# Three parts of the second layer's adaption in a one-core block kernel: summed by VectorE among the attention heads instead of by TensorE

## What is computed

```python
def second_block(x, c, w_ada, b_ada, norm_g, ...):
    c_act = jax.nn.silu(c)                                   # one row of 1024
    for layer in range(DEPTH):
        ada = jnp.einsum('bd,de->be', c_act, w_ada[layer]) + b_ada[layer]      # 3072 numbers
        shift, scale, gate = jnp.split(ada, 3, axis=-1)
        h = rms_norm(x, norm_g[layer]) * (1.0 + scale[:, None, :]) + shift[:, None, :]
        y = even_mixer(h, ...) if layer % 2 == 0 else odd_mixer(h, ...)
        x = x + gate[:, None, :] * y
    return rms_norm(x, final_g)
```

## Time and profile before

| | before |
|---|---|
| median of three runs (lowest, highest) | 1607.51 us (1602.76, 1608.37) |
| the profiled execution | 1602.8 us |
| its span, first to last instruction | 1600.9 us |
| TensorE busy in the span | 1573.0 us (98%) |
| VectorE busy | 875.0 us (55%) |
| ScalarE busy | 454.7 us (28%) |
| mean granted clock of TensorE, share of full | 0.999 |
| bytes moved by DMA | 243.40 MB, mean 152 GB/s |

### The profile page before, as it was taken

The page is one execution under the profiler, slowest core; times in us unless marked ns, Lnnn a source line. Parts: engine busy times, 40 slices in busy tenths (PEclk is TensorE's granted clock), DMA queues, the critical chain, the costliest instruction groups (busy, mean ns, idle before and its releaser), DMA issues.

```text
span 1600.9 us, 25330 instructions
## 1 busy us (share of the span) xinstructions
PE 1573.0 (98%) x10283; PEld 1353.5 (85%) x10283; DVE 875.0 (55%) x1685; ACT 454.7 (28%) x949; POOL 11.5 (1%) x24
## 2 busy tenths in 40 slices
PE   7999999999999999999999999999999999999998
PEld 6878868888899999878876888799999777678887
DVE  5547782222667774455793331566775573535663
ACT  5344323212200001335423301310011464623431
POOL 0000000000000000100000000000000000000000
PEclk9999999999999999999999999999999999999999
DMA  9443352342585455333343343485454834473420
GB/s 297 156 154 105 105 173 94 132 158 65 174 285 162 146 163 194 122 118 106 128 146 109 114 149 105 158 255 167 152 172 152 272 119 158 156 253 124 153 106 27
DMA packets 172373, 243.40 MB, mean 152 GB/s; under 512 B 16830, under 2 KB 95204, under 8 KB 172260
## 3 DMA queue, kind: packets, MB, share of 16 engines
q1 hardware_dynamic: 170660, 238.65, 44.3%
q10 hardware_dynamic: 1600, 3.15, 0.6%
HBM read 240.72 MB, written 1.05 MB: 151 GB/s over the span
## 4 chain that ended last, share of the span: by engine, by line
PE 96%; DVE 1%; ACT 1%; issue 1%; DMA 0%; SPq 0%; DVEq 0%; POOL 0%; ACTq 0%
PE psum L599 45%; PE psum L1408 26%; PE psum L610 4%; PE psum L2558 3%; PE psum L411 2%; PE psum L1184 2%; PE psum L2648 2%; PE psum L444 1%; PE psum L1262 1%; PE psum L427 1%; PE psum L2656 1%; PE psum L1234 1%; PE psum L2515 1%; PE psum L633 1%; PE psum L1219 1%
## 5 line engine op out<-in xcount | busy, mean ns | idle before, releaser
L599 PE MATMUL psum<-hT,ring 128*128 128x256 f32 x2448 | 540.8, 380 | 6.0 <-ACT hT L2755 2.6
L599 PEld LDWEIGHTS psum<-hT,ring 128*128 128x128 f32 x2448 | 461.2, 190 | 77.9 <-issue 15.1
L482 DVE TENSOR_TENSOR psum<-psum,const 128x512 f32<-128x512 f32 (+3 forms) x39 | 22.0, 582 | 123.3 <-PE psum L411 118.1
L599 PE MATMUL psum<-uT,ring 128*128 128x256 f32 x384 | 85.6, 381 | 0.0
L1408 PE MATMUL psum<-hT,ring 128*128 128x128 f32 x704 | 82.3, 275 | 2.7 <-issue 2.7
L1408 PEld LDWEIGHTS psum<-hT,ring 128*128 128x128 f32 x704 | 80.4, 192 | 3.1 <-issue 3.1
L599 PEld LDWEIGHTS psum<-uT,ring 128*128 128x128 f32 x384 | 72.5, 190 | 10.9 <-issue 0.7
L1668 ACT ACTIVATE SCR<-SCR 128x512 f32<-128x512 f32 x22 | 13.9, 630 | 220.9 <-DVEq L2166 220.9
L460 ACT ACTIVATE SCR<-psum,stats 128x128 f32<-128x128 f32 (+2 forms) x128 | 49.5, 398 | 55.2 <-DVE stats L496 55.0
L1440 ACT ACTIVATE G<-psum 128x512 f32<-128x512 f32 x32 | 19.1, 597 | 124.8 <-PE psum L599 124.8
L1926 DVE COPY_PREDICATED SCR<-levels,psum 128x512 f32<-128x512 uint8 x32 | 23.4, 733 | 56.7 <-PE psum L1184 56.0
(11 more groups left out here) (512 smaller groups left out, 2574.4 us busy)
## 6 DMA issues: line engine op xcount, KB each, us to landing
ring<-in_w_in SPq DMA_DIRECT2D x46, 1024.0 KB, 7.3
ring<-in_ffn_w_gate_up SPq DMA_DIRECT2D x88, 512.0 KB, 6.0
ring<-in_w_ada SPq DMA_DIRECT2D x24, 1024.0 KB, 9.9
ring<-in_ffn_w_down SPq DMA_DIRECT2D x16, 1024.0 KB, 7.0
ring<-in_w_in_odd SPq DMA_DIRECT2D x16, 1024.0 KB, 8.4
ring<-in_w_in_even SPq DMA_DIRECT2D x10, 1024.0 KB, 7.3
ring<-in_x_w_kv SPq DMA_DIRECT2D x8, 1024.0 KB, 6.0
ring<-in_ssm_w_glu SPq DMA_DIRECT2D x8, 1024.0 KB, 6.3
```

The source lines that it names most:

```text
L482: ins = nc.vector.tensor_tensor(pick(view), pick(view), mask[:, heads], ALU.add)
L599: ins = nc.tensor.matmul(b[0:width, n * S:n * S + S], w[k // 4][:, k % 4, c0[n]:c0[n] + width], tile(k), start=k == 0, stop=k == kt - 1)
```

## The change

TensorE's eight matmuls for each of the three parts go, as do ScalarE's copies. Instead VectorE multiplies each of the eight tiles of a part's matrix (128 x 512) by its column of `c_wide`, one number per partition, and adds it to a row of 128 x 512 in SBUF: the first tile with one tensor_scalar, the other seven with scalar_tensor_tensor (`sum_ada`, one half of a part at a time). Each instruction waits for the one before it. The halves stand in VectorE's steps 10, 11, 12, 13 and, two of them, 14, ahead of what else stands at the end of these steps. TensorE then sums over the 128 partitions with four matmuls whose moving side is one column of ones (`ada_total`, 128x1), in the places of the transposes, and VectorE adds the bias (`store_ada`). The ring's slots of the three parts are freed by the job za3 and by the sums' semaphore.

```diff
-           7: ["zb1", "zb2"], 8: ["zb3", "silu b"], 9: ["za0"], 10: ["za1"], 11: ["ada11"], 12: ["za2", "part ada11"],
-           13: ["za3", "silu a"], 14: ["ada12", "ada13"], 15: ["part 0", "part ada12", "part ada13"],
+           7: ["zb1", "zb2"], 8: ["zb3", "silu b"], 9: ["za0"], 10: ["za1"], 12: ["za2", "part ada11"],
+           13: ["za3", "silu a"], 15: ["part 0", "part ada12", "part ada13"],
...
+ADA_SUMS = {10: [(1, 0)], 11: [(1, 1)], 12: [(2, 0)], 13: [(2, 1)], 14: [(3, 0), (3, 1)]}
...
     for n in (1, 2, 3):
-        ada(1, n)
+        wide(f"ada1{n}", a["w_ada_2"], 512 * n, 512, "za3", 1)
...
+        def ada_total(n):
+            b = ojobs.begin(pe, f"ada1{n} turned")
+            pe.wait_ge(sig["ada_summed"], 2 * n)
+            row = m["ada_rows"][(6 + n) % ADA_SLOTS]
+            for i in range(4):
+                ins = nc.tensor.matmul(b[:, i:i + 1], row[:, i * P:(i + 1) * P], ones[:, 0:1], start=i == 0, stop=i == 3)
+            ins.then_inc(ojobs.done, 1)
...
-                elif name.startswith("ada"):
-                    n = int(name[4])
-                    ada_copy(1, n, {1: None, 2: None, 3: "04"}[n])
...
+        def sum_ada(n, h):
+            w = ring.arrived(dve, f"ada1{n}.{h}")
+            row = m["ada_rows"][(6 + n) % ADA_SLOTS]
+            for k in range(4):
+                by = m["c_wide"][:, 4 * h + k, 0:1]
+                if h == k == 0:
+                    link(V.tensor_scalar(row, w[:, k, :], by, None, ALU.mult))
+                else:
+                    link(V.scalar_tensor_tensor(out=row, in0=w[:, k, :], scalar=by, in1=row, op0=ALU.mult, op1=ALU.add))
+            dve.sem_inc(sig["ada_summed"], 1)
+
+        def store_ada(n):
+            name = f"ada1{n} turned"
+            b = ojobs.full(dve, name)
+            at = ROWS["b_ada"][0] + 4 * n
+            ojobs.release(V.tensor_tensor(ada[:, 24 + 4 * n:28 + 4 * n], b[:, 0:4], m["par"][1][:, at:at + 4], ALU.add),
+                          name)
+            ojobs.evacuated(dve, name)
...
+            for n, h in ADA_SUMS.get(i, []):
+                sum_ada(n, h)
             if i == 12:
-                ada_store(V, dve, link, m, ojobs, 1, 1)
+                store_ada(1)
             if i == 14:
                 gated(z[:, 0:4, :], a_out, 2, *(f"a heads{c}" for c in range(4)))
             if i == 15:
                 for n in (2, 3):
-                    ada_store(V, dve, link, m, ojobs, 1, n)
+                    store_ada(n)
...
+        summed |= {f"{DEPTH} ada1{n}.{h}": (second["ada_summed"], 2 * (n - 1) + h + 1) for n in (1, 2, 3) for h in range(2)}
```

More of the change, by code:

```diff
@@ L2577, in ab_fill @@
                     continue
[L2578 to L2581, removed]
+                if name.startswith("part ada"):
+                    ada_total(int(name[9]))
                 elif name.startswith("part"):
```

## The result

| | before | after |
|---|---|---|
| median of five runs each on one chip (lowest, highest) | 1604.13 us (1602.51, 1608.37) | 1617.14 us (1614.62, 1617.83) |
| ratio to before, 95% interval | 1 | 1.0067 [1.0054, 1.0080] |
| the profiled execution; its span | 1602.8; 1600.9 us | 1617.14; 1615.3 us |
| mean granted clock of TensorE | 0.999 | 0.990 |

The change makes the kernel slower by 0.67%, 10.8 us. A second series of the same kernel gave 1616.85 us and 1.0067 [1.0055, 1.0079]. The plain distance of the medians is 13.0 us here, with five runs of before that spread over 5.9 us, and 11.1 us in the second series.

What follows compares the result with a forecast made beforehand. It took TensorE as the bound before, and VectorE's closed-up row as what makes part 0 late: 7.4 + 1.0 (totals) + 1.7 (clock) = +10.1 us, 1612.9 for the profiled execution, 1617.6 us as median (+0.63%), range 1608 to 1622.

Steps and rivals of the forecast that it cites:

- VectorE's row, 7.4 us: VectorE's blocks and sums close up from step 11 on, so part 0 starts 7.4 us late, 1404.2 against 1396.8.
- the 0.4 for ten joints: End of VectorE's row before part 0: some ten joints between blocks at 0.04 us each, 1403.8 to 1404.2.
- the 0.03 and 0.11 in the sums: VectorE's sums: 0.03 us more per dependent instruction start, and 0.11 us for each half's closing semaphore increment.
- rival 2: VectorE's sums cheaper than priced, 18 instructions saving 0.27 us each; clock holds; +3.5 us, 1611.0 us; chance 0.10.
- The clock at part 0, 1.7 us: TensorE idles before part 0, whose first 3.4 us then run at half clock: 1.7 us lost, bounds 0 and 3.4.
- Rival 1: VectorE's row holds but TensorE's clock doesn't fall before part 0: +8.4 us, 1615.9 us; chance 0.20.
- The totals, 1.0 us: Behind part 0 on TensorE, one-column matmuls for parts 2 and 3 replace transposes, adding 1.0 us in full.
- TensorE's saving, nothing: TensorE's work falls by 3.9 us taken alone, but it can't use this while part 0 waits.
- The rival that let it stand: TensorE's 3.9 us saving stands, 1603.6 us, if VectorE's row ends before 1396.8 and part 0's weights come sooner; chance 0.06.
- The weights of part 0, "0.4 us earlier at best": Part 0's weights land near 1396.2, so even without VectorE's delay it could start only 0.4 us earlier.
- with late weights alone it is +0.6: If VectorE's row no longer delays part 0 but its weights still land late, the kernel is 0.6 us slower.
- if VectorE waits among these blocks: Sign of a wrong prediction: VectorE was to have no wait from 1373 to 1402.

Runs made afterwards that it cites:

- experiment 2: Changed kernel plus thirteen 128x256 matmuls on TensorE in the wait before part 0: 1615.98 us, ratio 1.0060 against the kernel before.
- Experiment 5: Kernel before plus VectorE's 24 sum instructions into a row nobody reads, TensorE's old matmuls kept: 1615.46 us, ratio 1.0061.
- experiment 4: Changed kernel with sums in steps 7 to 11, za2, za3 and silu a one step earlier, part 2's total before part 0: 1608.73 us, ratio 1.0014.
- experiment 7: As experiment 4, plus eight unread 128x128 matmuls on TensorE ahead of the turning of unit 12: 1603.84 us, ratio 0.9988 against the kernel before.
- experiment 1: Changed kernel without the arithmetic of VectorE's 24 sum instructions, totals kept: 1612.27 us, ratio 1.0035 against the kernel before.
- experiment 6: As experiment 1, plus fifteen matmuls of no use in three TensorE waits: 1606.19 us, ratio 1.0000 against the kernel before.
- experiment 3: Changed kernel with all six halves of the sums moved to VectorE's steps 7 to 11: 1613.89 us, ratio 1.0050 against the kernel before.

## Why the prediction was right, and where its reasons were not

It forecast 1617.6 us, slower; the median is 1617.14. That the two are only 0.5 us apart is in part luck. The level that it started from, a median of 1607.51, was some 1.4 us too high (1605.8 to 1606.4 in the later series), and its +10.1 us were somewhat too few (10.8 by the ratio, 11.1 by the medians of the second series). Within the 10.1, too much for VectorE and too little for the clock cancel. By its own steps, between the landmarks:

- **VectorE's row, 7.4 us: 6.9 measured** (part 0 31.5 us after the scores of unit 11, before 24.6). The parts hold: scalar_tensor_tensor in this form takes 0.75 us and starts every 0.78, the tensor_scalar 0.48, VectorE has no wait above 0.43 us from step 11 on in the first profile. The 0.5 us too much are almost all the 0.4 for ten joints: the lengths of the blocks, read from start to end, and the 0.03 and 0.11 in the sums held these gaps already. In the second profile it has waits, 1.0 and 0.8 us in steps 12 and 13 (shown below). The groups of the trace after, by shape (count | busy us, mean ns | idle before):

```profile
L3002 DVE SCALAR_TENSOR_TENSOR bT<-ring,c_wide,bT 128x512 f32<-128x512 f32 x14 | 10.5, 751 | 0.6
...
L3000 DVE TENSOR_SCALAR bT<-ring,c_wide 128x512 f32<-128x512 f32 x2 | 1.0, 476 | 0.0
```

  The neighbour in the earlier trace rows was right to the nanosecond, and rival 2 falls with it. The halved rate that the Vector Engine (DVE) Microarchitecture Reference of the Trainium skill (Points that are easy to get wrong) gives for two such SBUF sources isn't seen here either: 751 ns with both sources in SBUF, 751 with one in PSUM (L1959).
- **The clock at part 0, 1.7 us: 2.3 measured**, 2.8 in the second profile. Part 0 ran at half clock for 4.6 us and not for 3.4. Rival 1 falls, and experiment 2 shows the cause. The long wait was not what brought it down, though: it had fallen at 1399.1, behind the wait of 1.53 us. Experiment 5, where it fell only in the long wait, gives the same length of part 0, 7.55 us.
- **The totals, 1.0 us: 0.84 measured** (1.71 for 16 records, before 0.87), at 0.107 us per record.
- **TensorE's saving, nothing: right, and shown** by experiment 5. The rival that let it stand had its condition right (the row must end before part 0 could begin), and experiments 4 and 7 fulfil it.
- **The weights of part 0, "0.4 us earlier at best": right in kind, too early.** With VectorE out of the way part 0 did wait for them (experiment 1), and began 2.6 us later than before, counted from the scores of unit 11: 1.7 by za2's slow clock, 0.9 by later weights. With the clock up (experiment 6) it began 0.1 us later than before.
- **The step that failed: "with late weights alone it is +0.6".** Experiment 1 gave +5.6, and experiment 6 shows why. The sentence took the emptied places on TensorE to be free once VectorE was out of the way. I had asked of the clock only at the one long wait, and let the row of 1.8 us without a fall stand for all short ones. Behind waits of 1.45 to 1.8 us in steps 12 and 14 it came down as well, and za2, the heads and part 0 then run at half speed. In the kernel after, part of this lay in the shadow of VectorE's row: za2 took 1.5 us more in the first profile, and VectorE still did not wait for it. In the second it took 2.4 more, and VectorE waited for TensorE, for the total of part 1 and for the scores of unit 13:

```profile
1386.79 0.16 DVE L3009 TENSOR_TENSOR ada<-psum,par 128x4 f32<-128x4 f32 x1 [1.00 <-PE psum L2582]
1387.75 0.70 DVE L482 TENSOR_TENSOR psum<-psum,const 128x512 f32<-128x512 f32 x1 [0.80 <-PE psum L411]
```

  In these rows a slow clock reaches VectorE's row, which is 1.6 us longer there; experiment 2 has two such waits too (1.08 and 0.80 us, za2 3.0 us slower). The sum of the prediction had no term for it, and its own sign of being wrong, "if VectorE waits among these blocks", is there in one profile of the two.

So of the 10.8 us, 5.2 go when the sums' arithmetic goes, and the other 5.6 go when TensorE's waits are then filled: in the main the lowered clock, which becomes visible only then. In the kernel after the two overlap: they can't be given shares of a sum, only an order of removal.

The median of before fell from 1607.51 to 1604.13 us with the two runs that were added to the three shown ahead. That did not touch the forecast of 1617.6 us. The ratio, 0.67%, is near the 0.63% forecast.

## What to carry to other kernels

An idle stretch on a helper engine counts only between the two points that wait for it: add up that engine's blocks with the new work and compare the end with the time at which the bound engine wants the result, before counting what the bound engine saves. Taking work off TensorE in places where it then waits may cost more than the work did (here 5.6 us for 5.4), since the clock falls and the work behind runs at half speed; fill the place with other real work, and see that no wait is left beside it (experiments 4 and 7), or keep the old work there. When a removed cost leaves a loss, put work back into the idle places to find out whether it is the clock.

## What the runs showed of the hardware that was not expected

- **Short waits lower TensorE's clock, but not each time.** The wait of 1.45 us in step 12 was followed by a fall in all four profiled executions that have it (za2 took 5.0 us in the kernel after, 6.0 in its second profile, 5.2 and 6.6 in experiments 1 and 2, instead of 3.6). A wait of 1.76 to 1.77 us at L599, some 40 us earlier and in code that all kernels share, was followed by a fall to 0.5 to 0.6 in seven of the ten profiled executions (both of the kernel after, experiments 1, 3, 4, 6 and 7), and by none in the kernel before and in experiments 2 and 5, with the same idle time. What decides is not in these rows, and I leave it open. The TensorE: Matmul & The Clock Gate page of the Trainium skill (HAM oscillation — how this bites in real kernels) ties the fall to long idle gaps; four falls out of four behind 1.45 us of idle, beside three executions without one behind 1.77, don't fit a rule of a gap's length alone.
- **One such fall costs 1.4 to 3.0 us** (1.4 and 1.7 behind that wait at L599, in the two profiles of the kernel after; 2.7 in the first 25 us of the program, from the distance of the two traces; 1.5 to 3.0 at za2; 1.5 to 2.8 at part 0). They come and go between executions: near 18 us the second profile of the kernel after has a clock of 1.00 from 17 to 23 us, where the first has half. This fits the spread of the times (1602.5 to 1608.4 us before); that they are all of it was not tried.
- **A record of a one-column matmul costs as much as one of a transpose of 128x128, and a float32 matmul has two:** 16 records of 128x1 (8 matmuls) in 1.71 us, 0.107 each, and 8 of the old transposes, one record each, in 0.87, 0.109 each.
